# Delta rule in a transformer kernel: one form of the inverse made from the other by transposes, the coupling moved between partition halves by DMA, modulation products in other gaps

## The reference, cut to what matters

```python
decay = jnp.exp(jnp.where(tril, gc[..., :, None] - gc[..., None, :], -jnp.inf))
m = jnp.where(strict, jnp.einsum('bhncd,bhnsd->bhncs', kb, kc) * decay, 0.0)
tmat = lax.linalg.triangular_solve(m + eye, jnp.broadcast_to(eye, m.shape), left_side=True,
                                   lower=True, unit_diagonal=True)
u = jnp.einsum('bhncs,bhnsv->bhncv', tmat, vb)
w = jnp.einsum('bhncs,bhnsk->bhnck', tmat, kb * jnp.exp(gc)[..., None])
...
def step(s, inp):
    u_i, w_i, qk_i, qd_i, kd_i, gl_i = inp
    v_new = u_i - jnp.einsum('bhck,bhkv->bhcv', w_i, s)
    o_i = jnp.einsum('bhck,bhkv->bhcv', qd_i, s) + jnp.einsum('bhcs,bhsv->bhcv', qk_i, v_new)
    s = s * gl_i[..., None, None] + jnp.einsum('bhck,bhcv->bhkv', kd_i, v_new)
    return s, o_i
```

## Time and profile before

| | us |
|---|---|
| median of 3 runs | 2209.3 (2207.96 to 2212.66) |
| profiled execution, its own time | 2210.5 |
| its span | 2208.7 |
| first level products of pair 0 to the last output of pair 3 | 198.5 to 421.0 |
| TensorE busy over the span | 2134.0 (97%) |
| VectorE / ScalarE / GpSimd busy | 57% / 22% / 6% |

### The profile page before, as it was taken

The page is one execution under the profiler, slowest core; times in us unless marked ns, Lnnn a source line. Parts: engine busy times, 40 slices in busy tenths (PEclk is TensorE's granted clock), DMA queues, the critical chain, the costliest instruction groups (busy, mean ns, idle before and its releaser), DMA issues.

```text
span 2208.7 us, 36553 instructions
## 1 busy us (share of the span) xinstructions
PE 2134.0 (97%) x15690; PEld 1532.7 (69%) x15690; DVE 1256.9 (57%) x2205; ACT 477.3 (22%) x987; POOL 139.1 (6%) x148
## 2 busy tenths in 40 slices
PE   6999999999999999999999999999999999999998
PEld 3447877554688886457466995687795488769646
DVE  2675545377744546652356776485776428666643
ACT  2433211252300000022162110223220022411101
POOL 0003323000000000003010000002000000200000
PEclk9999999999999999999999999999999999999999
DMA  8221444413422223446102444332344443334441
GB/s 331 77 76 40 155 155 156 164 39 154 170 96 77 96 78 133 173 150 153 63 15 96 172 172 172 143 115 112 137 172 172 153 148 120 115 118 170 172 175 73
DMA packets 41679, 290.07 MB, mean 131 GB/s; under 512 B 5040, under 2 KB 6448, under 8 KB 7216
## 3 DMA queue, kind: packets, MB, share of 16 engines
q1 hardware_dynamic: 39344, 279.99, 34.5%
q0 software_dynamic: 1312, 3.15, 1.1%
q10 hardware_dynamic: 864, 4.61, 0.5%
HBM read 286.15 MB, written 1.05 MB: 130 GB/s over the span
## 4 chain that ended last, share of the span: by engine, by line
PE 91%; DVE 4%; ACT 2%; issue 1%; DMA 1%; SPq 0%; ACTq 0%; DVEq 0%
PE banks L998 22%; PE banks L1525 16%; PE banks L1714 12%; PE banks L2868 6%; PE banks L2211 6%; PE banks L412 5%; PE banks L1894 2%; PE banks L1918 2%; PE banks L778 2%; PE banks L638 2%; PE banks L1914 1%; PE banks L2862 1%; PE banks L450 1%; PE banks L793 1%; PE banks L784 1%
## 5 line engine op out<-in xcount | busy, mean ns | idle before, releaser
L998 PE MATMUL banks<-arena 128*128 128x512 f32 x392 | 186.2, 593 | 0.7 <-DVE arena L1770 0.5
L998 PE MATMUL banks<-weight_ring,arena 128*128 128x512 f32 x338 | 156.8, 593 | 0.0
L998 PEld LDWEIGHTS banks<-arena 128*128 128x128 f32 x392 | 74.2, 190 | 93.5 <-issue 92.2
L1525 PE MATMUL banks<-normed,weight_ring 128*128 128x128 f32 x1040 | 130.3, 282 | 2.5 <-DVE normed L555 1.3
L2868 PE MATMUL banks<-normed,weight_ring 128*128 128x256 f32 x576 | 130.9, 388 | 1.2 <-DVE normed L555 0.6
L1525 PEld LDWEIGHTS banks<-normed,weight_ring 128*128 128x128 f32 x1040 | 125.4, 198 | 3.5 <-issue 3.2
L2211 PE MATMUL banks<-normed,weight_ring 128*128 128x512 f32 x288 | 126.1, 593 | 0.0
L963 DVE TENSOR_TENSOR arena<-weight_ring 128x512 f32<-128x512 f32 x67 | 46.2, 690 | 136.8 <-PE banks L998 136.7
L2868 PEld LDWEIGHTS banks<-normed,weight_ring 128*128 128x128 f32 x576 | 111.2, 195 | 18.5 <-issue 2.5
L998 PEld LDWEIGHTS banks<-weight_ring,arena 128*128 128x128 f32 x338 | 63.6, 190 | 76.3 <-issue 75.6
L1525 PE MATMUL banks<-normed,arena 128*128 128x128 f32 x960 | 116.0, 275 | 0.0
(11 more groups left out here) (479 smaller groups left out, 3849.2 us busy)
## 6 DMA issues: line engine op xcount, KB each, us to landing
weight_ring<-in_weights SPq DMA_DIRECT2D x266, 1024.0 KB, 4.8
residual<-in_tokens ACTq DMA_DIRECT2D x1, 2048.0 KB, 12.6
mix<-in_rpb POOLq DMA_DIRECT2D x32, 64.0 KB, 3.6
constants<-in_const ACTq DMA_DIRECT2D x1, 1953.5 KB, 12.7
out<-residual SPq DMA_DIRECT2D x1, 1024.0 KB, 4.8
branch<-arena POOLq DMA_DIRECT2D x1, 512.0 KB, 4.8
normed<-in_ple POOLq DMA_DIRECT2D x1, 512.0 KB, 3.5
vector_params<-in_vectors ACTq DMA_DIRECT2D x1, 223.0 KB, 5.6
```

Source lines behind the costliest of these rows:

```text
L998: return pe.matmul(self.bank[i], left, b, start=(p == 0), stop=(p == n - 1))
L1525: mm = pe.matmul(o, a[:, k * P:k * P + P], right[:, k], start=(k == 0), stop=(k == H - 1))
```

## The change

Four things are changed in `delta_stage`:

1. The product Y.T PR (`g_px`) and its subtraction on VectorE are gone, and so are the 16 small transposes of level 0. Instead `across` makes X from Y: four 128x128 transposes for each u (each turns two heads of both chunks), and ScalarE copies the bank to `X[u]`. It runs after level 0 and after lv 1 to 4, behind the subtraction that makes Y.
2. A 128x128 transpose puts head p of a pair of heads in partition half p, with the two chunks side by side. So `X[u]` is laid out by head in the halves, no longer by chunk, and the level product needs the masked levels in the same layout. VectorE therefore writes the coupling to `L[u][1]`, and ScalarE issues four DMAs for each u (`move`) that copy its quarters into `C[u]` with the halves exchanged as needed: 64 partitions of 1 KB each, 64 KB a DMA, 512 KB a pair. GpSimd takes level 0 from `L[u][1]` as it is and levels 1 to 5 from the moved `C[u]`.
3. The level product reads one half of the partitions and writes, in turn, both halves: the matrices of one chunk and one head go to bank 2u+p.
4. The modulation pieces of pairs 0, 2 and 3 go between the transposes of u = 0 and of u = 1 at lv 2, 3 and 4, and `spread` to that place at lv 1. Pair 1 has one piece there at lv 4 and two at lv 5 where they were.

```diff
+        def across(j, lv, between=None):
             for u in range(2):
-                pe.wait_ge(sg["g_level"].sem, at["g_level"] + per["g_level"] * j + u + 1)
-                for m in range(8):
-                    for n in range(2):
-                        mm = pe.matmul(heads(2 * u + 1)[halves[n], m, :], L[u][0][halves[n], m, :], K.c("ident")[halves[n], halves[n]], start=True, stop=True)
-                mm.then_inc(sg["g_lv0"].sem, 1)
+                if u and between:
+                    between()
+                pe.wait_ge(sg["g_y"].sem, at["g_y"] + per["g_y"] * j + 2 * lv + u + 1)
+                y = Y[u].rearrange("p h n -> p (h n)")
+                for i in range(4):
+                    mm = pe.transpose(K.bank(2 * u + 1)[:, i * P:i * P + P], y[:, i * P:i * P + P], K.c("ident"))
+                mm.then_inc(sg["g_across"].sem, 1)
...
+            beside = {lv: (lambda k=lv - 2: fills[j].product(pe, k, k + 1)) for lv in (2, 3, 4)} if j != 1 else {4: first_piece}
+            beside[1] = lambda: spread(j)
             for lv in range(1, 6):
...
-                    for m in range(8):
+                    for h in range(HEADS):
+                        p, i = h % 2, h // 2
                         for n in range(2):
-                            mm = pe.matmul(heads(2 * u)[halves[n], m, :], L[u][lv % 2][halves[n], m, :], X[u][halves[n], m, :], start=True, stop=True)
+                            mm = pe.matmul(K.psum[halves[n], 2 * u + p, 64 * i:64 * i + 64], L[u][lv % 2][halves[p], 4 * n + i, :], X[u][halves[p], 2 * i + n, :], start=True, stop=True)
                     mm.then_inc(sg["g_prod"].sem, 1)
...
-                    if lv < 5:
-                        for m in range(8):
-                            for n in range(2):
-                                mm = pe.matmul(heads(2 * u)[halves[n], m, :], Y[u][halves[n], m, :], PR[u][halves[n], m, :], start=True, stop=True)
-                        mm.then_inc(sg["g_px"].sem, 1)
...
+                if lv < 5:
+                    across(j, lv, beside.get(lv))
...
+        def move(j):
+            for u in range(2):
+                act.wait_ge(sg["g_c"].sem, at["g_c"] + per["g_c"] * j + u + 1)
+                for p in range(2):
+                    for n in range(2):
+                        act.dma_start(C[u][halves[p], 4 * n:4 * n + 4, :], L[u][1][halves[n], 4 * p:4 * p + 4, :]).then_inc(moved[u].sem, 16)
+
+        def take_across(j, lv):
+            for u in range(2):
+                act.wait_ge(sg["g_across"].sem, at["g_across"] + per["g_across"] * j + 2 * lv + u + 1)
+                act.activation(X[u], heads(2 * u + 1), ACT.Copy).then_inc(sg["g_x"].sem, 1)
...
             if j + 1 < NP:
                 decays(j + 1)
+                move(j + 1)
             fills[j].keep(act)
+            if j + 1 < NP:
+                take_across(j + 1, 0)
...
+                    elif lv == 1:
+                        pool.wait_ge(moved[u].sem, mv[u] + 64 * (j + 1))
+                        pool.wait_ge(sg["g_level"].sem, at["g_level"] + per["g_level"] * j + u + 1)
...
-                    if lv < 5:
-                        dve.wait_ge(sg["g_px"].sem,
-                                    at["g_px"] + per["g_px"] * j + 2 * (lv - 1) + u + 1)
-                        dve.tensor_tensor(out=X[u], in0=X[u], in1=heads(2 * u), op=ALU.subtract).then_inc(sg["g_x"].sem, 1)
```

More of the change, by code:

```diff
@@ L1824, in delta_stage @@
     gm, go = gram_made.reserve(4), gram_out.reserve(4)
+    moved = [K.counter(f"g_moved_{u}") for u in range(2)]
+    mv = [c.reserve(64 * NP) for c in moved]
     E, C, L, X, Y, PR = (B[n] for n in ("E", "C", "L", "X", "Y", "PR"))
@@ L1883, in spread, with first_piece @@
                 mm.then_inc(sg["g_spread"].sem, 1)
+        def first_piece():
+            pe.wait_ge(gram_out.sem, go + 4)
+            fills[1].product(pe, 0, 1)
         def levels(j):
+            beside = {lv: (lambda k=lv - 2: fills[j].product(pe, k, k + 1)) for lv in (2, 3, 4)} if j != 1 else {4: first_piece}
+            beside[1] = lambda: spread(j)
             for lv in range(1, 6):
@@ L1910, in levels @@
                     pe.wait_ge(sg["g_y"].sem, at["g_y"] + per["g_y"] * j + 2 * (lv - 1) + u + 1)
-                    if lv < 5:
-                        for m in range(8):
-                            for n in range(2):
-                                mm = pe.matmul(heads(2 * u)[halves[n], m, :], Y[u][halves[n], m, :], PR[u][halves[n], m, :], start=True, stop=True)
-                        mm.then_inc(sg["g_px"].sem, 1)
-                    for m in range(8):
+                    for h in range(HEADS):
                         for n in range(2):
-                            mm = pe.matmul(heads(2 * u + 1)[halves[n], m, :], PR[u][halves[n], m, :], Y[u][halves[n], m, :], start=True, stop=True)
+                            mm = pe.matmul(heads(2 * u + 1)[halves[n], h, :], at_head(PR[u], h)[halves[n]], Y[u][halves[n], h, :], start=True, stop=True)
                     mm.then_inc(sg["g_py"].sem, 1)
+                if lv < 5:
+                    across(j, lv, beside.get(lv))
         def solve(j):
@@ L1932, in turned @@
                         p, i = h % 2, h // 2
-                        mm = pe.matmul(K.psum[halves[p], (1, 4)[u] + n, 64 * i:64 * i + 64], ke[halves[n], 64 * h:64 * h + 64], at_head(Y[u], h)[halves[n]], start=True, stop=True)
+                        mm = pe.matmul(K.psum[halves[p], (1, 4)[u] + n, 64 * i:64 * i + 64], ke[halves[n], 64 * h:64 * h + 64], Y[u][:, h, :][halves[n]], start=True, stop=True)
                     return mm
@@ L1937, in solve @@
                     for n in range(2):
-                        pe.matmul(K.bank(3 * u)[halves[n], 64 * h:64 * h + 64], at_head(Y[u], h)[halves[n]], vtok[halves[n], tile(j, u), 64 * h:64 * h + 64], start=True, stop=True)
+                        pe.matmul(K.bank(3 * u)[halves[n], 64 * h:64 * h + 64], Y[u][:, h, :][halves[n]], vtok[halves[n], tile(j, u), 64 * h:64 * h + 64], start=True, stop=True)
                 turned(1).then_inc(sg["g_uw"].sem, 1)
@@ L2029, in scalar @@
                     grams(2)
+                if lv < 5:
+                    take_across(j, lv)
             for u in range(2):
@@ L2064, in gpsimd @@
                                      at["g_prod"] + per["g_prod"] * j + 2 * (lv - 3) + u + 1)
-                    pool.tensor_tensor(out=L[u][lv % 2], in0=C[u], in1=bc(level[:, 6 * d + lv, :], 1, 8), op=ALU.mult).then_inc(sg["g_level"].sem, 1)
+                    mask = level[:, 6 * d + lv, :]
+                    if lv:
+                        ins = pool.tensor_tensor(out=L[u][lv % 2], in0=C[u], in1=bc(mask, 1, 8), op=ALU.mult)
+                    else:
+                        ins = pool.tensor_tensor(out=L[u][0].rearrange("p (i q) n -> p q i n", q=2), in0=L[u][1].rearrange("p (q i) n -> p q i n", q=2), in1=bc(bc(mask, 1, 4), 1, 2), op=ALU.mult)
+                    ins.then_inc(sg["g_level"].sem, 1)
                 if lv == 1:
@@ L2101, in first_level @@
                 dve.tensor_tensor(out=Y[u], in0=ident, in1=L[u][0], op=ALU.subtract).then_inc(sg["g_y"].sem, 1)
-            for u in range(2):
-                dve.wait_ge(sg["g_lv0"].sem, at["g_lv0"] + per["g_lv0"] * j + u + 1)
-                dve.tensor_tensor(out=X[u], in0=ident, in1=heads(2 * u + 1), op=ALU.subtract).then_inc(sg["g_x"].sem, 1)
         def levels(j):
```

29 lines of the change are left out of this document (10 added, 19 removed).

## The result

| | us |
|---|---|
| before | 2209.3 (2208.0 to 2214.3, 5 runs beside those of after) |
| after | 2223.5 (2214.9 to 2226.1, 5 runs) |
| ratio | 1.0053, 95% interval 1.003 to 1.0075 |
| forecast | 2206, range 2197 to 2219, slower by over 0.2%: 0.25 |

The change costs 14 us. The time is outside the range, on the slow side. The profiled execution of after is its fastest, 2214.9. Its mean clock is 0.988, against 0.981 to 0.985 in the other four. So its trace accounts for about 5 us of the 14, and the rest can't be read in it.

What follows compares the result with a forecast made beforehand. TensorE, busy 97% of the span, was taken to bound the kernel. Levels -12.8, start -0.2, issues +6.6 and landing +3.0 summed to -3.4 us, giving 2206 after the 1.2 offset to the runs' median; range 2197 to 2219.

Steps and rivals of the forecast that it cites:

- Levels, -12.8: Delta stage levels: pairs 0, 2 and 3 save 3.3 us each, pair 1 saves 2.9, together 12.8.
- Rival (c): Delta stage levels shorten by 6 us instead of 12.8, waits replacing TensorE's work: 2213; chance 0.12.
- The mode switch: TensorE between 64x64 and 128x128 work: the drain is already in the measured distances, so the sum stays the same.
- Start of pair 0, -0.2: Before pair 0's levels: transposes take 1.2 against 1.9 us, but X waits behind eight DMA issues; net -0.2 us.
- Eight issues between pairs, +6.6: ScalarE between pairs: eight issues at 0.44 us delay `keep` and `turn` by 2.2 each; 4.4 to 8.7 by issue cost.
- Landing, +3.0: Moves between pairs land behind weights, making the masked level late by 1.0 us in each of three passages.
- rival (b): Between pairs, moves crawl behind weights and land after 257, each pair 4 to 5 us late: 2216, to 2221; chance 0.20.
- the 1.6: TensorE's clock after a wait: 4 us at the fallen rate of 0.59 lose about 1.6 us; counted only in rival (b).
- `turn` later: Sign of being right, after the last scan product: eight ScalarE issues of 0.44 us and `turn` 2.2 us later.
- GpSimd's mask waiting for a DMA: Sign of being right: GpSimd's second mask waits on a DMA in the profile after.
- Clock near 0.5 between pairs: Sign of being wrong: TensorE's clock near 0.5 between pairs in the profile after.
- TensorE over 3 us for a masked level: Sign of being wrong: TensorE waits over 3 us for a masked level between pairs.

Runs made afterwards that it cites:

- e8: e3, but pair 0's moves issued by ScalarE as in the changed kernel, those of pairs 1 to 3 on SyncE; 2197.7 us, ratio 0.9949 to before.
- e4: The kernel before plus eight dummy 64 KB DMAs issued by ScalarE at the moves' places, landing not needed for 20 us; 2226.0 us, ratio 1.008.
- e2: The changed kernel with ScalarE's `keep` ahead of the eight DMA issues between pairs; 2213.8 us, ratio 1.0021 to before.
- e5: As e3, but between pairs the moves are issued on SyncE two weight loads later; 2202.4 us, ratio 0.9967 to before.
- e3: The changed kernel with all 32 moves issued by SyncE ahead of weight loads, none by ScalarE; 2191.3 us, ratio 0.9921 to before.
- e6: e3 with the modulation pieces and `spread` back at their places in the kernel before; 2202.6 us, ratio 0.9972 to before.

## Why the prediction was wrong, step by step

**Levels, -12.8.** In sum right: -13.4. The parts weren't. A level was 0.36 shorter than worked out (5.59 for 5.95), since the product block takes 0.56 at most and not 0.80, and its consumer starts after 0.77 and not 1.06: I priced it by the Gram matrices and not by its own pattern. The undisturbed pair 2 took 26.8 and not 28.45. What this gave was lost in pairs 0 and 3 to the wait at the start, a clock of 0.63 and holes. Rival (c) fell.

**The mode switch.** The fill starts 0.58 after the four transposes of u = 0 begin (216.31 to 216.89), where the forecast had 0.60 with the drain in it. The Trainium skill, "TensorEngine Tiling (Array Packing)", Key Properties, has the switch drain TensorE; nothing had to be added for it.

**Start of pair 0, -0.2.** Wrong: +2.2 to the first product, and 2.6 of waiting for the moves of u = 1 after it. e8 gives 6.4 in all, with the clock. The forecast named the wait of X behind eight issues and then gave it no term, though eight issues at its own 0.44 are 3.5.

**Eight issues between pairs, +6.6.** The mechanism was right and the size wrong, and this is the step that failed. The delay of `turn` was to be 2.2 a passage. Measured, TensorE waited 3.85, 4.04 and 4.53 there, and the scans grew by 4.4, 3.9 and 5.5: 13.8 in all for a term of 6.6. Three things are in it. An issue takes 0.62 and not 0.44 (5.16 to 5.78 for eight against 3.5, +1.7 to +2.3 each time). TensorE's wait of 3.9 to 4.5 brings a clock fall (the windows from `turn` to the end of each passage lose 1.7, 1.7 and 3.6, together 7.0 of the 12.0). And my bound of 8.7 from 0.53 an issue was no upper bound: the row that would have made it one, the store at 0.627, was in the trace before, and I took the six issues of ScalarE because they were on the same engine. The 32 issues by GpSimd (L2750), the only long row of them in that trace, have a median of 0.644. e4 shows the term alone, with the start and the passages behind it: +17.

**Landing, +3.0.** The forecast had the moves of u = 1 land near 258. They took 7.2 to 9.8 between pairs 0 and 1; the last one was issued at 251.5 and landed at 259.3, and GpSimd starts on u = 0 at 258.68. But in after this lies under the delay of `keep`: the masks are ready before TensorE asks for them. The passages' +5.8 is the clock, and the Y that VectorE makes more slowly beside GpSimd. e2 shows what they cost when nothing covers them: passages of 10 for 5, +5 each, the size that rival (b) had given (4 to 5). The Trainium skill, "DMA: Bandwidth & Descriptors", Queues, rings and completion order, has each engine serve its queues in turn. The landings agree in direction: 2.0 while the weights pause (pair 0), 7.7 in the median of all 32. How packets of two queues alternate isn't shown by these runs, and in e5 the moves stand in the weights' own queue and still take 3.7 to 8.0 between pairs. That page's advice against transfers to partition halves, in Rules for kernel authors, was not tested.

**Rival (b)** had the right sign and nearly the size (2216 to 2221 for 2223.5), and its condition, a landing after 257, was met. But its mechanism, TensorE waiting for the landing, is not what after's trace shows; the slow side came by the issues. That the number lies near (b) is luck. I had given all slow cases 0.25, because each cost was taken at its middle and the clock's part stood in a rival and not in the sum. A wait of 4 us on an engine that is busy otherwise should have carried the 1.6 that the forecast itself had worked out from the earlier trace rows; with that, the waits as measured (4.1 in the mean) and the start, the sum is -12.8 + 6.4 + 3 x (4.1 + 1.6) = +10.7, and +13.7 with the 3.0 for the landing, which `keep` covers. That is near the 14.2 measured, though it is arithmetic after the fact, and only 4.4 to 6.6 of the 14.2 can be followed in after's trace. The rest stays open.

**Said and seen.** `turn` later: yes, by twice as much. GpSimd's mask waiting for a DMA: yes. Clock near 0.5 between pairs: yes (0.50 at 372), named as the sign of being wrong. TensorE over 3 us for a masked level: not in after, 5.0 in e2. Holes over 0.4: five for four, 3.9 in sum for 4.9.

## What to carry to other kernels

Starting a DMA takes time of the engine that issues it: count 0.6 us each, as here for small ones in a row, and ask what is queued behind it. Then put it on a queue whose next work has slack, and ahead of the bulk loads: e3 and e5 issue the moves between pairs 0 and 1 at the same moment, and their place before or behind two loads in each pair from 1 on is worth 11 us. Where TensorE is otherwise never idle, a wait of a few us costs itself and, here, 1.7 to 3.6 more in clock. Price an operation by the row with the same shape or the worst like row on any engine, not by the rows of the engine that happens to do it.

## What the runs showed of the hardware that was not expected

- Eight DMA issues in a row took 0.62 each on ScalarE, for 4 KB as for 64 KB, for 64 as for 128 partitions, from SBUF as from HBM, and 0.60 on SyncE for the 64 KB moves; a 1 MB weight load takes 0.33.
- The one 64 KB move that was issued together with a 1 MB load landed after 5.3 (after) and 5.2 (e8), its seven siblings after 2.0.
- A 64x64 product that reads one half of the partitions and writes both, with four quadrants taking turns, ran 32 rows in at most 0.56, against 0.93 for products within the two diagonal quadrants.
- Holes of 0.4 to 2.2 us, in which TensorE waits for nothing that the trace shows, come in before, after, e3 and e6, at other places in each. With the fills moved they went from 9.3 in sum to 5.5 (e6, e3). Their cause isn't known from these runs.
- The same program ran at mean clocks of 0.981 to 0.988 and times of 2215 to 2226 (after), while e3, without a clock fall in the stage, stayed within 1.2 us in four runs. That the spread comes from the clock falls is likely by this, but only one execution of each was traced.
